# Squares for the residual norms: from ScalarE to GpSimd, with TensorE's column sums kept in one piece

## The reference, cut to what matters

```python
for i in range(DEPTH):
    sh1, sc1, g1, sh2, sc2, g2 = _ada(c, ada_w[i], ada_b[i])
    hx = _modulate(_rmsnorm(x, norm1_g[i]), sh1, sc1)
    yx = _mla(hx, ...) @ w_o  or  _fourier_mix(hx, fno_w)
    x = x + g1 * yx
    x = x + g2 * _conv_ffn(_modulate(_rmsnorm(x, norm2_g[i]), sh2, sc2), ...)
return _rmsnorm(x, final_norm_g)

def _rmsnorm(x, g):
    y = x * rsqrt(mean(x * x, axis=-1) + NORM_EPS)
    return y * g
```

## Time and profile before

| | |
|---|---|
| runs | 2248.65, 2244.56, 2217.69 us |
| median | 2244.56 us |
| the profiled execution's own time | 2248.65 us, its span 2246.8 us |
| mean granted TensorE clock | 0.974 of 2.4 GHz |
| busy: TensorE, VectorE, ScalarE, GpSimd | 97%, 76%, 52%, 3% of the span |
| squares on ScalarE (L685) | 64, from 401 to 419 ns each |
| adds on GpSimd (L454) | 56, from 737 to 2070 ns each |
| DMA | 547.01 MB, mean 243 GB/s |

### The profile page before, as it was taken

The page is one execution under the profiler, slowest core; times in us unless marked ns, Lnnn a source line. Parts: engine busy times, 40 slices in busy tenths (PEclk is TensorE's granted clock), DMA queues, the critical chain, the costliest instruction groups (busy, mean ns, idle before and its releaser), DMA issues.

```text
span 2246.8 us, 46018 instructions
## 1 busy us (share of the span) xinstructions
PE 2170.3 (97%) x17426; PEld 2091.6 (93%) x17426; DVE 1702.0 (76%) x1955; ACT 1172.0 (52%) x1591; POOL 75.7 (3%) x64
## 2 busy tenths in 40 slices
PE   7898999999999999999999999989999999999997
PEld 3577999899999999999999989989999999999997
DVE  6856887889888888788878876998886664456665
ACT  6874454434666666433345544456666663334553
POOL 0000000011000000000000120200000000000002
PEclk9999999999999999899999999999999999999999
DMA  9863665678677777699968761967765555555553
GB/s 352 309 211 113 219 225 203 217 290 329 227 279 280 280 280 279 234 373 371 369 228 288 278 214 51 379 247 280 278 235 193 179 188 175 189 195 190 194 190 129
DMA packets 127799, 547.01 MB, mean 243 GB/s; under 512 B 14576, under 2 KB 15088, under 8 KB 107248
## 3 DMA queue, kind: packets, MB, share of 16 engines
q1 hardware_dynamic: 127728, 546.03, 67.9%
HBM read 543.88 MB, written 2.10 MB: 243 GB/s over the span
## 4 chain that ended last, share of the span: by engine, by line
PE 91%; DVE 6%; ACT 2%; issue 1%; DMA 1%; POOL 0%; ACTq 0%; DVEq 0%; SPq 0%
PE bank L1282 25%; PE bank L1284 25%; PE bank L1283 25%; PE bank L1318 2%; PE bank L1288 2%; PE bank L1290 2%; PE bank L1289 2%; PE bank L1358 2%; DVE w_lo L842 1%; PE bank L1516 1%; PE bank L1344 1%; PE bank L1374 1%; PE bank L1375 1%; PE bank L1376 1%; DVE w_lo L787 1%
## 5 line engine op out<-in xcount | busy, mean ns | idle before, releaser
L469 ACT CAST w_hi<-raw 128x1024 fp32r<-128x1024 f32 x624 | 652.4, 1050 | 530.8 <-PE bank L1284 492.7
L787 DVE TENSOR_TENSOR w_lo<-raw,w_hi 128x1024 fp32r<-128x1024 f32 x624 | 770.6, 1246 | 181.2 <-ACT w_hi L469 181.1
L1282 PE MATMUL bank<-h_hi,w_hi 128*128 128x256 f32 x3152 | 886.7, 281 | 14.3 <-DVE w_lo L787 9.3
L1283 PE MATMUL bank<-h_lo,w_hi 128*128 128x256 f32 x3152 | 884.9, 281 | 0.0
L1284 PE MATMUL bank<-h_hi,w_lo 128*128 128x256 f32 x3152 | 884.8, 281 | 0.0
L1282 PEld LDWEIGHTS bank<-h_hi,w_hi 128*128 128x128 f32 x3152 | 596.9, 189 | 15.0 <-issue 15.0
L1283 PEld LDWEIGHTS bank<-h_lo,w_hi 128*128 128x128 f32 x3152 | 601.2, 191 | 0.3 <-issue 0.2
L1284 PEld LDWEIGHTS bank<-h_hi,w_lo 128*128 128x128 f32 x3152 | 600.7, 191 | 0.0
L1282 PE MATMUL bank<-a_hi,w_hi 128*128 128x256 f32 x1408 | 394.2, 280 | 3.3 <-DVE a_lo L791 2.0
L1283 PE MATMUL bank<-a_lo,w_hi 128*128 128x256 f32 x1408 | 393.4, 279 | 0.0
L1284 PE MATMUL bank<-a_hi,w_lo 128*128 128x256 f32 x1408 | 393.4, 279 | 0.0
(11 more groups left out here) (199 smaller groups left out, 2472.6 us busy)
## 6 DMA issues: line engine op xcount, KB each, us to landing
raw<-weights SPq DMA_DIRECT2D x626, 512.0 KB, 4.7
ada<-ada_late SPq DMA_DIRECT2D x160, 1024.0 KB, 4.9
early<-weights SPq DMA_DIRECT2D x72, 512.0 KB, 5.8
kv_raw<-kv_weights SPq DMA_DIRECT2D x8, 512.0 KB, 7.4
ctx_s<-ctxT SPq DMA_DIRECT2D x4, 512.0 KB, 5.3
x<-xT SPq DMA_DIRECT2D x4, 512.0 KB, 8.4
outT<-h_pre SPq DMA_DIRECT2D x4, 512.0 KB, 2.6
dft_s<-dft SPq DMA_DIRECT2D x1, 768.0 KB, 8.1
```

The costliest lines, as they stand in the source:

```text
L469: act.copy(w_hi[:, slot, :], raw[:, slot, :]).then_inc(hi_done, 1)
L787: dve.tensor_tensor(w_lo[:, slot, :], raw[:, slot, :], w_hi[:, slot, :].bitcast(f32), ALU.subtract)\
L1282: pe.matmul(out, wh, hi_part, start=first, stop=False)
L1283: pe.matmul(out, wh, lo_part, start=False, stop=False)
```

## The change

ScalarE's `residual_square` is gone, and its `square` is a loop of casts alone. GpSimd's `residual_squares` now makes each square as `x * x` (a tensor_tensor multiply) right ahead of the add that uses it, waiting for the residual itself. The square of the last tile is its last instruction in each round. On TensorE `gap_sums` and `acc_columns` are gone; in rounds 0 and 2 the norm sum now comes first and the 16 columns behind it in one piece, as in round 1.

```diff
@@ gpsimd
-            def residual_squares(round_, after):
+            def residual_squares(Y0, round_, after):
                 pool.wait_ge(*after)
                 t0, a0 = KT * round_, SQ_ADDS * round_
+                def square_of(m, s):
+                    pool.wait_ge(y_free, 2 + Y0 + m + 1)
+                    xm = row(x, m)
+                    pool.tensor_tensor(sqt[:, s, :], xm, xm, ALU.mult).then_inc(sqt_done, 1)
+                def add(m, s):
+                    pool.wait_ge(sqt_done, t0 + m + 1)
+                    pool.wait_ge(sq_done, a0 + m)
+                    pool.tensor_tensor(sq[:, 0:SEQ], sq[:, 0:SEQ], sqt[:, s, :], ALU.add).then_inc(sq_done, 1)
+                square_of(0, 0)
                 pool.wait_ge(sqt_done, t0 + 1)
                 pool.tensor_copy(sq[:, 0:SEQ], sqt[:, 0, :]).then_inc(sq_done, 1)
                 for m in range(1, KT - 1):
-                    pool.wait_ge(sqt_done, t0 + m + 1)
-                    pool.wait_ge(sq_done, a0 + m)
-                    pool.tensor_tensor(sq[:, 0:SEQ], sq[:, 0:SEQ], sqt[:, m % 2, :], ALU.add).then_inc(sq_done, 1)
+                    if m > 1:
+                        pool.wait_ge(sq_done, a0 + m - 1)
+                    square_of(m, m % 2)
+                    add(m, m % 2)
+                square_of(KT - 1, 1)
@@ scalar
-            def residual_square(Y0, round_, after, m):
-                if m == 0:
-                    act.wait_ge(*after)
-                elif m > 1:
-                    act.wait_ge(sq_done, SQ_ADDS * round_ + m - 1)
-                act.wait_ge(y_free, 2 + Y0 + m + 1)
-                act.activation(sqt[:, m % 2, :], row(x, m), ACT.Square).then_inc(sqt_done, 1)
-            def square(c0, Y0, round_, after):
+            def square(c0):
                 load_sqrt()
-                for m in range(KT):
-                    split(c0 + 2 * m + 4, c0 + 2 * m)
-                    if m:
-                        residual_square(Y0, round_, after, m - 1)
-                    split(c0 + 2 * m + 5, c0 + 2 * m + 1)
-                residual_square(Y0, round_, after, KT - 1)
+                with act.Fori(0, KT // 2) as i:
+                    for e in range(4):
+                        split(c0 + 4 * i + 4 + e, c0 + e)
@@ scalar, end of ffn
-                m = 0
                 for c in range(c3 + 4, c3 + 28):
                     if c < N_CHUNKS:
                         split(c, c)
-                    if 2 * (c - c3 - 4) >= 3 * (m + 1):
-                        residual_square(Y0 + KT, 2 * layer + 1, (norm_summed, after), m)
-                        m += 1
-                for m in range(m, KT):
-                    residual_square(Y0 + KT, 2 * layer + 1, (norm_summed, after), m)
@@ tensor
-            def gap_sums(round_, b):
-                acc_columns(b, 0, range(KT // 2))
-                residual_sum(round_)
-                acc_columns(b, 0, range(KT // 2, KT)).then_inc(ada_summed, 1)
@@ tensor, after square(C_WO, ...); the same after square(C_FNO, ...)
-            gap_sums(0, B_WO)
+            residual_sum(0)
+            ada_sum(B_WO)
```

More of the change, by code:

```diff
@@ L451, in residual_squares @@
                 for m in range(1, KT - 1):
-                    pool.wait_ge(sqt_done, t0 + m + 1)
-                    pool.wait_ge(sq_done, a0 + m)
-                    pool.tensor_tensor(sq[:, 0:SEQ], sq[:, 0:SEQ], sqt[:, m % 2, :], ALU.add).then_inc(sq_done, 1)
[L456 to L459, removed]
+                    if m > 1:
[3 more added lines that the diff above has]
+                square_of(KT - 1, 1)
+            residual_squares(Y_WO, 0, (o_taken, 1 + HEADS))
+            residual_squares(Y_FFN0 + KT, 1, (norm_summed, NRM_L0F + 1))
+            residual_squares(Y_FNO, 2, (norm_summed, NRM_L1 + 1))
+            residual_squares(Y_FFN1 + KT, 3, (norm_summed, NRM_L1F + 1))
         @block.scalar
@@ L704, in normed, with ffn @@
                         between(m)
-            def ffn(c0, T0, P0, Y0, layer, after):
+            def ffn(c0, T0, P0, layer):
                 def pair(c, T, Pn, f, j, s):
@@ L742, in ffn @@
                         split(c, c)
-                    if 2 * (c - c3 - 4) >= 3 * (m + 1):
-                        residual_square(Y0 + KT, 2 * layer + 1, (norm_summed, after), m)
-                        m += 1
-                for m in range(m, KT):
-                    residual_square(Y0 + KT, 2 * layer + 1, (norm_summed, after), m)
-            square(C_WO, Y_WO, 0, (o_taken, 1 + HEADS))
+            square(C_WO)
             normed(4, H_L0F, SH2)
-            ffn(C_FFN0, T_UP0, 0, Y_FFN0, 0, NRM_L0F + 1)
+            ffn(C_FFN0, T_UP0, 0, 0)
             def spectrum(g):
@@ L775, in _ @@
                 fourier(g)
-            square(C_FNO, Y_FNO, 2, (norm_summed, NRM_L1 + 1))
+            square(C_FNO)
             normed(6, H_L1F, 6 + SH2)
-            ffn(C_FFN1, T_UP1, FT, Y_FFN1, 1, NRM_L1F + 1)
+            ffn(C_FFN1, T_UP1, FT, 1)
             std(7, SEQ)
@@ L1311, in lat_sum, with ada_sum @@
                 mm.then_inc(norm_summed, 1)
-            def acc_columns(b, n, columns):
+            def ada_sum(b):
                 pe.wait_ge(ada_used, ADA_AT[b + 1])
[L1316 to L1322, removed]
                 for n in range(ADA_BLOCKS[b][1]):
-                    mm = acc_columns(b, n, range(KT))
+                    acc = (acc0, acc1)[n]
+                    for j in range(KT):
+                        mm = pe.matmul(bank[7][:, n * KT + j:n * KT + j + 1], acc[:, j * P:(j + 1) * P],
+                                       ones[:, 0:1], start=True, stop=True)
                 mm.then_inc(ada_summed, 1)
@@ L1684, in _ @@
             square(C_FNO, Y_FNO, f_hi, f_lo)
-            gap_sums(2, B_FNO)
+            residual_sum(2)
+            ada_sum(B_FNO)
             ffn(C_FFN1, T_UP1, FT, Y_FFN1, H_L1F, 1)
```

## The result

| | before | after |
|---|---|---|
| median of the runs | 2229.74 us (20 runs) | 2249.55 us (20 runs) |
| lowest, highest | 2217.54, 2248.65 | 2234.88, 2265.14 |
| the profiled execution, its span | 2248.65, 2246.8 | 2254.86, 2253.1 |
| ratio after to before | | 1.0076, 95% interval 1.0052 to 1.0100 |

The change makes the kernel slower by 0.76%, some 17 us. More runs of the kernel before were made beside the changed one, and its median came down from 2244.56 to 2229.74 us: the execution that was profiled is the slowest of the twenty.

A forecast was written before the change was run, and what follows sets the result against it. TensorE, 97% busy, dominates the chain, but a full VectorE ends rounds 0 and 2. Two rounds at 13.8 us, -1.6 (round 1) and +0.3 (round 3) give +26.3 us on the 2244.56 us median: 2271 us, range 2244 to 2288.

The forecast's parts named there:

- The level: Whole kernel: the starting time, median 2244.56 us (profiled execution 2248.65), to which the summed changes were added.
- the squares of rounds 0 and 2: One-tile stages: GpSimd squares stretch a tile to 6.03 us from 5.45, costing 8.1 us in each round.
- What bounds the stage: Rounds 0 and 2: VectorE, not TensorE, already sets the end; last residual starts 1.1 us after TensorE's last-tile columns start.
- The price of a square: Rounds 0 and 2: one GpSimd instruction inside a full VectorE queue costs VectorE 0.55 us; bounds 0 and 0.74.
- The last square and the norm sum: End of rounds 0 and 2: last square on GpSimd +1.2 us, norm sum at the slow clock +0.3 us, each round.
- The columns: Gap behind rounds 0 and 2: 16 columns behind the norm sum take 6.83 us, delaying `mods` by 4.2 us each round.
- Round 1: Long down-projection end: last square, norm sum and columns come earlier, -1.6 us; bounds +1 and -4 us.
- Round 3: Long down-projection end: last square takes 0.74 us in place of 0.42, +0.3 us; VectorE's idle half covers the rest.
- Rival C: Gaps of rounds 0 and 2: locks as forecast, but columns at the fast clock; 2265 us, chance 0.18.
- A: Rounds 0 and 2: squares are free, the 0.55 us not billed; +2 us in all, 2247 us, chance 0.10.
- B: Round 1's norm gap closes, columns at full clock there, -4.7 us, squares free elsewhere; 2240 us, chance 0.04.
- D: One-tile stages: TensorE's clock falls, a tile takes 10.9 us instead of 6.03; +58 us, 2329 us, chance 0.06.

## Why the prediction was right or wrong, point by point

**The level.** The forecast started from the median of three runs, 2244.56 us, and the profiled execution at 2248.65. Twenty runs give 2229.74. The forecast of 2271 us is 21 us above the measured 2249.55, and 15 us of that is the base: here the prediction fails as a time, though the range holds it. The other 6.6 us is the sum: 26.4 us forecast, 19.8 between the medians, 17 by the ratio and 18.2 by the marks. So two steps failed: the level that the sum was added to, and, within the sum, the squares of rounds 0 and 2, put at 8.1 us a round and measured at 5.42 and 4.97. The spread of 31 us between three runs stood in the table; it was used for the range only. A window of an up-projection beside one of round 2, as in the section above, would have shown that the profiled execution was a slow one for a reason that has nothing to do with the change.

**What bounds the stage.** Right. VectorE sets the end of rounds 0 and 2; with its adaLN steps cut, the squares cost nothing (pitch 5.44 and 5.65 us in either kernel). But it was close: at TensorE's faster pace the kernel before went from 5.45 and 5.47 us to 5.44 when VectorE was relieved, and gained the rest, some 0.8 us, behind the last tile.

**The price of a square.** The mechanism was right, the term was mis-sized, and this is the largest error of the sum. Forecast 0.55 us a tile, taken from the add; measured 0.37 (5.83 against 5.46). Of the 0.18 us between, 0.13 comes of the square reading one tile: GpSimd needs 0.47 us once it is let in, and the add 0.60; with two tiles read the same extra multiply costs 0.49. The last 0.06 us is that an adaLN step grows by less than a split behind the same 0.60 us; why, is open. Round 0 lost 5.42 and round 2 4.97 us up to the last residual where 8.1 and 8.1 were forecast. This is 5.8 us of the 8.2 by which the sum of 26.3 was too high. The lower bound had been put at 0 and the upper at 0.74, and the nearest row was the wrong one in the number of tiles read. At TensorE's slow pace the price is smaller still, 5.83 against 5.65. The forecast also had TensorE waiting late in both stages: in round 0 no such wait shows, in round 2 none over 0.4 us.

**The last square and the norm sum.** Forecast 1.2 + 0.3 us a round, measured 1.62 and 1.61.

**The columns.** Forecast +4.2 us a round at the slow clock, measured 3.92 and 4.00, with 16 columns in 6.83 and 6.82 us. Rival C, the fast clock, did not come. Putting the columns back gave 3.4 us a round.

**Round 1.** Forecast -1.6, measured -3.57. The sum came 1.70 us earlier as said; the term that was left at its bound, the columns' clock behind a shorter gap, brought another 1.9 us (4.79 us for the columns in place of 6.83; 3.63 to 6.04 in the other profiles, so how much of it comes is luck of the execution). It lay within the bounds of +1 and -4.

**Round 3.** Forecast +0.3, measured +0.18. ScalarE's 26 us were put at nothing; the 0.6 us or more by which round 1 is shorter up to its last residual speaks against that, but no experiment took the squares off ScalarE alone.

**The rivals.** A (squares free) is right only where VectorE has room. B fell with it. D, the clock falling inside the stage, did not happen; but TensorE has a second pace at full granted clock, which no rival named.

**The size.** The forecast of 1.2% lies above the interval of 0.52 to 1.00%. That it would be slower, and by less than 2%, was right. The upper end of the range, 17 us above the forecast, is explained by terms that add up to 15.

## What to carry to other kernels

Before work is moved to an idle engine, look at what it shares with the full one: a GpSimd instruction that reads SBUF cost VectorE 0.36 to 0.55 us here, of 0.61 to 0.74 us of its own length, while VectorE's queue of two-input instructions was full, and nothing that counted when there was room, so the same move lost 5 us in one stage and gained 3.6 in another. Take the price from an instruction with the same number of tiles read. And work put into a gap of TensorE belongs ahead of the late result, not behind it, as long as it is done before that result comes: here the granted clock fell to 0.50 in the gap, and the columns behind it took 6.83 us in place of 3.63.

## What had not been expected of the hardware

- TensorE's matmuls of 256 columns come every 0.113 or 0.118 us at the same granted clock, constant through nearly every loop of these traces, different between executions of one kernel.
- GpSimd's product of a tile with itself takes less than its add of two tiles: 0.61 and 0.74 us with VectorE idle (round 3 of the changed kernel, below), 0.47 and 0.60 us once let in beside a full VectorE.

```profile
2231.43 0.61 POOL L454 TENSOR_TENSOR sqt<-x 128x256 f32<-128x256 f32 x1 [1.74 <-DVE x L1100]
2232.12 0.74 POOL L459 TENSOR_TENSOR sq<-sq,sqt 128x256 f32<-128x256 f32 x1
```

- A GpSimd memset of 0.31 us passed beside VectorE's split without delay to either.
